# 16-bit slot comparisons with the token block innermost, attention waits by halves of the heads, turned attention outputs and turned router logits

## The reference

```python
# first block, for each of 3 groups (window, dilation), 8 heads of 64, blocks of 128 queries
logits = jnp.einsum('bdhnqc,bdhnkc->bdhnqk', qb, kb) * scale + bias[None, None, :, None]
logits = jnp.where(valid, logits, -jnp.inf)
m = jnp.max(logits, axis=-1)
p = jnp.exp(logits - m[..., None])
s = jnp.sum(p, axis=-1)
num = jnp.einsum('bdhnqk,bdhnkc->bdhnqc', p, vb)
# second block
x = x + g1 * _merge(p, attn_lat, four_lat, w_o_attn[l], w_fourier[l], w_out[l])
h2 = _modulate(_rms(x, norm2_g[l]), sh2, sc2)       # _modulate(h, shift, scale) = h * (1 + scale) + shift
# _expert_choice(h2, ...), 16 experts, each takes its cap = 128 best tokens
logits = jnp.einsum('btd,de->bte', h, w_r, preferred_element_type=jnp.float32)
aff = jax.nn.softmax(logits, axis=-1)
gate, idx = lax.top_k(jnp.swapaxes(aff, 1, 2), cap)
xe = jax.vmap(lambda hb, ib: hb[ib])(h, idx)
ye = jnp.einsum('becf,efd->becd', jax.nn.silu(a) * u, w_d) * gate[..., None].astype(h.dtype)
```

## Time and profile before

| | |
|---|---|
| time, median of 3 runs | 2952.6 us (2950.39 to 2957.13) |
| time of the profiled execution | 2939.17 us |
| its span | 2937.4 us |
| TensorE matmuls busy | 2706.2 us (92%) |
| VectorE busy | 1481.4 us (50%) |
| ScalarE busy | 1058.1 us (36%) |
| GpSimd busy | 378.6 us (13%) |
| slot comparisons (L3082) | 16, mean 1216 ns |
| bytes moved by DMA | 355.96 MB, mean 121 GB/s |

### The profile page before, as it was taken

The page is one execution under the profiler, slowest core; times in us unless marked ns, Lnnn a source line. Parts: engine busy times, 40 slices in busy tenths (PEclk is TensorE's granted clock), DMA queues, the critical chain, the costliest instruction groups (busy, mean ns, idle before and its releaser), DMA issues. The chain is left out here.

```text
span 2937.4 us, 40180 instructions
## 1 busy us (share of the span) xinstructions
PE 2706.2 (92%) x16278; PEld 2207.7 (75%) x16278; DVE 1481.4 (50%) x2201; ACT 1058.1 (36%) x1868; POOL 378.6 (13%) x360
## 2 busy tenths in 40 slices
PE   8999999999899998998799999998999999949997
PEld 5777777777677888797677778867888777838786
DVE  5225543333373414213845242027666664579997
ACT  4114411111223414215226322115666521227775
POOL 0005400000120000001301000013111011113431
PEclk9999999999999999998899999999999999969999
DMA  7554661212321202203634112210000064269997
GB/s 220 200 191 134 186 192 49 74 57 63 109 100 37 80 15 48 83 0 120 199 115 153 47 43 90 85 62 20 2 1 1 3 196 141 115 240 360 378 378 257
DMA packets 261859, 355.96 MB, mean 121 GB/s; under 512 B 54091, under 2 KB 173027, under 8 KB 260268
## 3 DMA queue, kind: packets, MB, share of 16 engines
q1 hardware_dynamic: 212700, 201.17, 21.6%
q0 software_dynamic: 33744, 127.05, 13.3%
q10 hardware_dynamic: 15232, 25.17, 2.4%
HBM read 281.25 MB, written 76.80 MB: 122 GB/s over the span
## 5 line engine op out<-in xcount | busy, mean ns | idle before, releaser
L230 PE MATMUL ps<-h_hi,st_w_lo 128*128 128x512 f32 x880 | 363.7, 413 | 14.1 <-PEq L821 5.7
L232 PE MATMUL ps<-h_hi,st_w_hi 128*128 128x512 f32 x880 | 346.5, 394 | 0.0
L231 PE MATMUL ps<-h_lo,st_w_hi 128*128 128x512 f32 x880 | 346.4, 394 | 0.0
L227 DVE TENSOR_TENSOR ew_lo<-wraw,ew_hi 128x1024 fp32r<-128x1024 f32 x192 | 223.0, 1217 | 9.0 <-ACT ew_hi L224 8.2
L230 PEld LDWEIGHTS ps<-h_hi,st_w_lo 128*128 128x128 f32 x880 | 167.6, 190 | 65.8 <-issue 34.1
L224 ACT ACTIVATE ew_hi<-wraw 128x1024 fp32r<-128x1024 f32 x192 | 191.6, 1057 | 21.5 <-DMA wraw<-w_e_gate 9.2
L232 PEld LDWEIGHTS ps<-h_hi,st_w_hi 128*128 128x128 f32 x880 | 166.9, 190 | 36.1
L231 PEld LDWEIGHTS ps<-h_lo,st_w_hi 128*128 128x128 f32 x880 | 167.6, 190 | 32.5 <-issue 2.4
L227 DVE TENSOR_TENSOR st_w_lo<-wraw,st_w_hi 128x1024 fp32r<-128x1024 f32 x64 | 90.7, 1417 | 179.5 <-ACT st_w_hi L224 178.8
L230 PE MATMUL ps<-h_hi,w_ring_lo 128*128 128x512 f32 (+1 forms) x336 | 134.7, 401 | 2.5 <-DVE h_lo L227 1.5
L231 PE MATMUL ps<-h_lo,w_ring_hi 128*128 128x512 f32 (+1 forms) x336 | 133.6, 398 | 0.0
(11 more groups left out here) (587 smaller groups left out, 6363.0 us busy)
## 6 DMA issues: line engine op xcount, KB each, us to landing
wraw<-w_in SPq DMA_DIRECT2D x98, 512.0 KB, 4.9
wraw<-w_e_gate SPq DMA_DIRECT2D x64, 512.0 KB, 12.6
wraw<-w_e_up SPq DMA_DIRECT2D x64, 512.0 KB, 14.0
wraw<-w_e_down SPq DMA_DIRECT2D x64, 512.0 KB, 13.4
mod_w<-w_mod POOLq DMA_DIRECT2D x12, 2048.0 KB, 9.5
gates<-st_zo ACTq DMA_DIRECT2D x48, 256.0 KB, 2.0
rw_in<-rw_scan POOLq DMA_DIRECT2D x8, 1280.0 KB, 6.4
wraw<-w_out SPq DMA_DIRECT2D x16, 512.0 KB, 5.4
```

The costliest lines, as they stand in the source:

```text
L227: return dve.tensor_tensor(dst, src, hi.bitcast(F32), ALU.subtract)
L230: pe.matmul(out, a[1], b[0], start=first, stop=False)
L231: pe.matmul(out, a[0], b[1], start=False, stop=False)
L232: return pe.matmul(out, a[0], b[0], start=False, stop=last)
```

## The change

There are three edits in one change.

- **Attention.** The bias, the maxima and the exponentials are told by halves: even heads, then odd heads (`biased`, `row_max`, counts of `sb`, `nm` and `exp` doubled). The transposed groups run by parity, so the first two can start when the four even exponentials are done. For tiles of two key blocks `output` now takes `v` as the stationary operand (64 columns, even and odd head in separate column halves of the array) and `pt` as the moving one; the output comes out turned, ScalarE copies it to `og` (`numerators`), four transposes turn it back (`back`), and ScalarE copies it once more (`by_token`). For tiles of one key block the product stays, and its copy moves from ScalarE to VectorE (`token_rows`).
- **Router.** The transposes take the rows of `x2` as soon as they are there. The products have `wf`, the router weights times the gain, 16 of 32 columns filled, as stationary operand in four column groups; ScalarE copies their four partial sums (`quarters`), and one product with `pick` adds them and turns the result back. The row's scale and a bias are applied in the routing block, in two more VectorE operations. The pipeline is two steps shorter.
- **Slots.** `slot` and `iota` are bf16, the eight token tiles are the innermost dimension of both and of `oh`. GpSimd spreads `iota` out from the loaded numbers. The stationary columns of `slot_sums` so lie 16 bytes apart.

```diff
-                dve.tensor_tensor(oh[:, e % 2, :, :], iota[:, :].unsqueeze(1).to_broadcast([P, NT, CAP]),
-                                  slot[:, :, e:e + 1].to_broadcast([P, NT, CAP]), ALU.is_equal
+                dve.tensor_tensor(oh[:, e % 2, :, :], iota[:, :, :],
+                                  slot[:, e, :].unsqueeze(1).to_broadcast([P, CAP, NT]), ALU.is_equal
...
+                            for m in range(4):
+                                for kb in range(2):
+                                    for a in range(2):
+                                        h = 2 * m + a
+                                        mm = pe.matmul(ps[HD * a:HD * a + HD, 7, m * P:(m + 1) * P],
+                                                       v[:, j - 1 + kb, h * HD:(h + 1) * HD], pt[:, j % 2, kb, a, m, :],
+                                                       start=(kb == 0), stop=(kb == 1))
...
+                            pe.wait_ge(sn["og"], bs["og"] + done[j] + 1)
+                            for m in range(4):
+                                tr = pe.transpose(ps[:, 7, m * P:(m + 1) * P], og[:, j % 3, m * P:(m + 1) * P], ident[:, :])
+                            tr.then_inc(sn["pv"], 1)
...
-                            pe.wait_ge(sn["exp"], bs["exp"] + j + 1)
                             for n in range(ngrp[j]):
-                                kb, par = n // 2, n % 2
+                                par, kb = divmod(n, nkey[j])
                                 w = gsum[j] + n
+                                pe.wait_ge(sn["exp"], bs["exp"] + 2 * j + par + 1)
...
+                            if j + 1 < NT:
+                                biased(dve, j + 1, 1)
+                            if j and nkey[j - 1] == 1:
+                                token_rows(j - 1)
+                            turned(j, 3 if nkey[j] == 2 else 1)
+                            if j + 1 < NT:
+                                row_max(dve, j + 1, 1)
...
+                        for k in range(KD):
+                            q_ = 32 * (k % 4)
+                            mm = pe.matmul(ps[q_:q_ + 32, 3, o:o + P], wf[:, k, :], ht[:, t % 2, k, :],
+                                           start=(k < 4), stop=(k >= 4))
+                        mm.then_inc(S("n4_part"), 1)
...
+                    link(dve.tensor_tensor(lg[:, :, :], lgp, wide(row_scale), ALU.mult))
+                    link(dve.tensor_tensor(lg[:, :, :], lg[:, :, :], ps[:, 3, P:P + NE].unsqueeze(1).to_broadcast([P, NT, NE]),
+                                           ALU.add))
```

More of the change, by code:

```diff
@@ L1660, in on_dve @@
                             dve.wait_ge(S("gn_stored"), 64)
[L1661 removed]
+                        for par in range(2):
+                            biased(dve, 0, par)
+                            row_max(dve, 0, par)
                 def gates_stored(kind, eng):
@@ L1677, in _, with pt_copied @@
                     def _(pe):
+                        def pt_copied(pe, w):
+                            j = max(x for x in range(NT) if gsum[x] <= w)
+                            n = w - gsum[j]
+                            x, place = ((0, 0), (1, 0))[n] if nkey[j] == 1 else ((1, 0), (0, 0), (0, 1), (1, 1))[n]
+                            pe.wait_ge(sn[f"pt{x}"], bs[f"pt{x}"] + done[j] + place + 1)
                         def output(j):
                             for x in range(2):
-                                pe.wait_ge(sn[f"pt{x}"], bs[f"pt{x}"] + gsum[j + 1] // 2)
+                                pe.wait_ge(sn[f"pt{x}"], bs[f"pt{x}"] + done[j + 1])
@@ L1688, in output @@
-                            mm.then_inc(sn["pv"], 1)
+                                pe.wait_ge(sn["og"], bs["og"] + done[j])
+                            if nkey[j] == 1:
+                                for h in range(HEADS):
+                                    mm = pe.matmul(ps[:, 7, h * HD:(h + 1) * HD], pt[:, j % 2, 0, h % 2, h // 2, :],
+                                                   v[:, j, h * HD:(h + 1) * HD], start=True, stop=True)
+                                mm.then_inc(sn["pv"], 1)
+                                return
@@ L1733, in _ @@
                                 numerators(j - 1)
-                            for n in range(0, ngrp[j], 2):
+                            for n in ((1, 2) if nkey[j] == 2 else (0,)):
+                                par, kb = divmod(n, nkey[j])
                                 w = gsum[j] + n
@@ L2946, in rows_io @@
                     gp.dma_start(wr[:, :, :], A["w_router_2"][0].rearrange("(k p) e -> p k e", p=P)).then_inc(S("n4_in"), 16)
-                    for s_ in range(NT + 2):
+                    gp.memset(wf[:, :, :], 0.0).then_inc(S("n4_wf"), 1)
+                    gp.wait_ge(S("n4_in"), 48)
+                    gp.wait_ge(S("n4_wf"), 1)
+                    gp.tensor_tensor(wf[:, :, 0:NE], wr[:, :, :], gains[:, 5, :].unsqueeze(2).to_broadcast([P, KD, NE]),
+                                     ALU.mult).then_inc(S("n4_wf"), 1)
+                    for s_ in range(NT + 1):
                         if s_ < NT:
```

249 lines of the change are left out of this document (145 added, 104 removed).

## The result

The changed kernel took 2912.45 us (median of 4 runs, 2904.89 to 2915.48), the kernel before 2951.49 us beside it (4 runs): a ratio of 0.9868, 95% interval [0.9833, 0.9902], a gain of 39 us where 24.5 were forecast. The profiled execution took 2915.48 us with a span of 2913.7, which is the 2914.7 forecast for it; that agreement is partly an accident, as the experiments show.

What follows compares the result with a forecast made beforehand. TensorE, with matmuls busy 92% of the span, was taken to bound the kernel. Attention -14, router -7 and slots -3.5 sum to -24.5 us, from the median 2952.6 to 2928 us; own range 2919 to 2937, overall range 2915 to 2942.

Steps and rivals of the forecast that it cites:

- the same gain from the median: Whole kernel: the 24.5 us gain, summed on a profiled execution 13 us below the median 2952.6, gives 2928 us from it.
- Attention, -14: Three attention groups: turned outputs and waits by halves gain 7, 5 and 2 us, 14 in all.
- what is gained ahead of 1149.07 turns into a longer wait there: Second attention group: the store freeing `og` stands behind unchanged DMAs, so gains ahead of that wait are lost.
- 3.3 + 2: Second attention group, behind the `og` wait: 3.3 us from three two-block tiles, 2 from shorter waits for exponentials.
- the waits of 1.25, some three, shrink, but VectorE takes over a copy of 0.69: Third attention group, with no two-block tiles: TensorE's waits for exponentials shrink, VectorE gains a copy; 2 us gained.
- Router, -7: From the last product with `w_out` to the routing block: product ends 4.2 us later, tail 11.2; 15.4 replaces 22.3 us.
- Slots, -3.5: Routing block: nine faster comparisons save 4.8 us, strided stationary loads add 0.8 and two added operations 0.5.
- no overlap of the column halves: Rival, attention: the turned product's column halves do not overlap; attention +1 us, time 2943 us; chance 0.1.
- unchanged comparisons: Rival, slots: the comparisons stay at 1.15 us, time 2933 us; chance 0.1.
- the strided loads: Rival, sums matmuls: 0.2 us more per stationary load erases the gain, 0.4 more gives 2976 us; chance 0.03.
- Larger gains: Rival: DMA has slack so the seven comparisons beside the experts count, and the router gives 9; 2922 us; chance 0.15.
- -17 and -9, and -11 and -3: Far and near ends for attention (-17, -11) and router (-9, -3), named as the source of the range 2919 to 2937.

Runs made afterwards that it cites:

- before_again: The kernel before, unchanged, profiled once more and timed against itself: ratio 1.001, median 2948.12 us.
- attention_only: The kernel before with the attention edit alone: ratio 0.9921 to the kernel before, median 2920.91 us.
- router_only: The kernel before with the router edit alone: ratio 0.9978 to the kernel before, median 2940.07 us.
- after_again: The whole change, unchanged, profiled once more and timed in more runs: 2910.92 us, ratio 0.9869 [0.9843, 0.9895] to the kernel before.
- before_look3: The kernel before, unchanged, one more execution with a profile: 2952.59 us, with 207.8 us from the first attention group to the second.

## Why the prediction was wrong

Lengths of stages from the timelines, in us; old attention 8 profiles, changed 5:

| | old, range and mean | changed, range and mean | difference | forecast |
|---|---|---|---|---|
| first group to second | 199.4 to 207.8, 202.6 | 190.8 to 192.3, 191.7 | -10.9 | -7 |
| second to third | 199.3 to 204.9, 202.5 | 190.1 to 197.0, 194.4 | -8.0 | -5 |
| third to the next product | 51.3 to 55.3, 54.0 | 48.6 to 51.2, 49.3 | -4.7 | -2 |

**The step that failed first** is "the same gain from the median". The profiled execution of before was one in which the clock stayed up at the end of the first group; the median lay 13 us higher because many executions are not like that. The distance was carried over as if it were a constant, and with the change a good part of it was gone: against executions with the full clock the first group gains 199.4 - 191.7 = 7.7, the forecast's 7, against the others 16.

**Attention, -14, was too small** in the other two groups as well. In the second, "what is gained ahead of 1149.07 turns into a longer wait there" held. The wait of 2.56 was that one execution's (0 to 0.7 in the seven later ones), but the maxima begin 18.6 to 21.0 us from the block's start with the old attention and 18.2 to 19.4 with the changed one, which then waits 1.2 to 2.3. Rows of before_again and attention_only, whose blocks begin at 1129.87 and 1122.01:

```profile
1148.68 2.29 DVE L1608 TENSOR_REDUCE og<-sc 128x8 f32<-128x2048 f32 x1 [0.33 <-DMA attn_groups<-og]
```
```profile
1140.24 1.22 DVE L1608 TENSOR_REDUCE og<-sc 128x4 f32<-128x1024 f32 x1 [1.17 <-DMA attn_groups<-og]
```

The term that was too small is what lies behind: from these maxima to the next product 41.7 to 47.1 us (mean 44.6) became 35.1 to 39.8 (37.6), 6.9 where 3.3 + 2 were counted. Part of that is the clock again, for which the forecast has no term. Windows of 20 us from 50 us behind the block's start, the same two:

```profile
1179.87:1199.87 20.00, 16.54 (x71) 14.54 (x72) 6.10 (x6) 7.16 (x13) 1.49 (x2) 0.66 0.41 127
```
```profile
1172.01:1192.01 20.00, 17.74 (x86) 14.44 (x82) 5.88 (x6) 6.32 (x8) 1.49 (x2) 1.00 0.70 197
```

The granted clock there is 0.57 to 0.83 in all eight old profiles and 0.91 to 1.00 in the five changed ones; how much of the 6.9 it makes is not separated. In the third group, "the waits of 1.25, some three, shrink, but VectorE takes over a copy of 0.69" missed that ScalarE is full there and that the copy leaves it. Within the first group the terms held: tiles 6.39 for 6.4, outputs 1.89 for 1.78; the price of doing only one half of the edit (7.05 or 8.07) was nowhere asked.

**Router, -7, was right**, by two errors that cancel: router_only's time says -6.5, and from the stage's first matmul to the routing block it takes 114.5 to 115.7 us in five profiles, 122.5 with the old router, -7.6. The last product ends only about 1 us later, not 4.2 (the stage with `w_out` takes 100.5 to 101.7 us in five profiles, 99.6 to 100.0 with the old router): a set of products takes 2538.68 - 2538.10 = 0.58, not 0.9. The tail is 13.7, not 11.2, since from the last row to the next block it takes 6.4 and not 2.9 + 0.4; with a store of 3.1 to 3.8, it is the change of blocks above all that was priced too low.

**Slots, -3.5, measured -2.2** ahead of the experts. Comparisons came out at 0.69 (0.62 forecast) and strided loads at 170 - 101 = 69 ns more each (53 forecast); the slot copy, now with a strided result, takes 0.72 in place of 0.29, which was not counted. The seven comparisons beside the experts gave nothing, as forecast.

**Of the rivals**, no overlap of the column halves is refuted by the 1.89 us, unchanged comparisons by 0.69; the strided loads cost a third of what would have decided. Larger gains came true, but not for the reasons given. The range's own ends do not follow from the terms named for them: -17 and -9, and -11 and -3, with -3.5 for the slots, give 2923 and 2935, not 2919 and 2937.

The stages add up to -23.6 - 7.6 - 2.2 = -33 us, and the measured gain is 31 to 46 by after_again's interval. Against the five old profiles without the fall alone the same sum is -29, against the three with it -41: an estimate from the means of these stages. The median of before, at 2951.49, stood close under the times of those three, and 39 were measured. That it stood there is luck: of 92 later executions of the kernel before 37 took under 2947 us and 49 over 2950, and a median of four falls on either side.

## What to carry to other kernels

Before a sum is set against a median, ask why the profiled execution stands where it does: further profiles of the same kernel show stages that differ by 8 us (three of eight here; the second profile alone did not), and the first group's rests of 0.83 us could cost 8. Two edits that each move a different engine out of the way can be worth little alone and much together, so that a loop in which three engines are within a few per cent of each other is costed with all edits in. A wait seen once is looked for in a second execution: it can be that execution's, while the point in time that sets it stays. A queue's order is the first thing to try when a store is what frees a buffer.

## What the hardware showed beyond that

The clock of TensorE fell for 20 us after rests of 0.83 us in some executions of one program and not in others; with the rests filled the times lost their upper cluster, and with the changed attention rests of 0.69 to 0.85 us were followed by no such fall in five profiles. The Trainium skill, page "TensorE: Matmul & The Clock Gate", section "HAM oscillation — how this bites in real kernels", has a kernel whose clock falls again in each of its waits for DMA between bursts of matmuls. The rows of before_look3 agree in that the fall follows a rest; here it is a wait of 0.83 us for ScalarE, and only three executions of eight show the fall. A 16-bit comparison of two SBUF operands went from 1.218 to 0.683 us only with both operands contiguous inside, and a stationary operand of 128 bf16 columns 16 bytes apart loaded in 170 ns in place of 101 (medians of 128 loads, the changed kernel and the kernel before).
